# Other start addresses in SBUF for the split activations and the large region: two lead-in buffers and seven unused parameter columns

## The reference

```python
h = rmsnorm(x, mix_pre_g) * (1.0 + sc1) + sh1
proj = h @ w_in                                       # 1024 x 10272
y_ssd = ssd_branch(z, xbc, dt_raw, ...) @ w_ssd_out
y_sc = short_conv_branch(sc_b, sc_c, sc_h, sc_conv_w) @ w_sc_out
x = x + gt1 * rmsnorm((g_ssd * y_ssd + g_sc * y_sc) @ w_o, mix_post_g)
h = rmsnorm(x, ffn_pre_g) * (1.0 + sc2) + sh2
u_gate, u_val = jnp.split(causal_dwconv(h @ w_up, ffn_conv_w, ffn_conv_b), 2, axis=-1)   # 1024 x 5632
x = x + gt2 * rmsnorm((silu(u_gate) * u_val) @ w_down, ffn_post_g)                       # 2816 x 1024
...
x = x + gate_a * ((g_a * o_a + g_b * o_b) @ w_o)      # second layer: o_a, o_b are the two attentions
x = x + gate_f * ((silu(gt) * val) @ w_down)
```

## Time and profile before

| what | before |
|---|---|
| median of 3 runs | 1115.75 us (1113.66 to 1116.21) |
| time of the profiled execution | 1113.12 us |
| its span, as the profile shows it | 1111.3 us |
| TensorE matmul busy (PE) | 1051.7 us, 95% |
| weight loads (PEld) | 993.7 us, 89% |
| GpSimd (POOL) / ScalarE (ACT) / VectorE (DVE) busy | 692.6 / 642.6 / 562.8 us |
| mean granted TensorE clock | 0.986 of full |

### The profile page before, as it was taken

One profiled execution on the slowest core, in us unless ns is written; L12 is line 12 of the kernel. 1 busy time (PEld: TensorE's weight loads), 2 busy tenths in 40 slices (PEclk: granted clock), 3 DMA queues, 4 the chain that ended last, 5 costly groups with the idle time before them and its releaser, 6 DMA issues.

```text
span 1111.3 us, 22886 instructions
## 1 busy us (share of the span) xinstructions
PE 1051.7 (95%) x8357; PEld 993.7 (89%) x8357; DVE 562.8 (51%) x1165; ACT 642.6 (58%) x1140; POOL 692.6 (62%) x306
## 2 busy tenths in 40 slices
PE   3999999999899989999999999998998889999998
PEld 2999999988789979999998999896665689999998
DVE  5877425589774454555423432495263724444400
ACT  3555754477764576666546557735576546666532
POOL 0787888812268847888786487660220065888795
PEclk9999999999999999999999999999899999999999
DMA  9988677656427855676677387567211033555463
GB/s 372 380 283 287 245 292 285 224 184 209 168 99 268 263 204 171 228 242 223 217 258 252 110 286 278 174 206 293 98 40 38 1 117 129 195 186 188 162 208 106
DMA packets 63650, 226.84 MB, mean 204 GB/s; under 512 B 6976, under 2 KB 8160, under 8 KB 63328
## 3 DMA queue, kind: packets, MB, share of 16 engines
q1 hardware_dynamic: 62384, 221.74, 57.1%
q10 hardware_dynamic: 1200, 4.23, 1.3%
HBM read 224.86 MB, written 1.08 MB: 203 GB/s over the span
## 4 chain that ended last, share of the span: by engine, by line
PE 67%; issue 16%; POOL 8%; ACT 3%; DMA 2%; DVE 2%; SPq 1%; POOLq 0%; ACTq 0%; DVEq 0%
PE psL L550 64%; POOL WL L503 8%; DMA R<-ada_w 1%; PE psS L550 1%; PE psO L550 1%; DMA ring<-wts 1%; SPq L405 1%; ACT WH L1042 1%; ACT R L1153 0%; ACT L1033 0%; ACT HR L1074 0%; SPq L390 0%; POOL R L530 0%; PE psS L839 0%; DVE HR L1649 0%
## 5 line engine op out<-in xcount | busy, mean ns | idle before, releaser
L503 POOL TENSOR_TENSOR WL<-ring,WH 128x1024 fp32r<-128x1024 f32 (+1 forms) x282 | 672.2, 2398 | 306.4 <-ACT WH L1042 245.5
L550 PE MATMUL psL<-HR,WH 128*128 128x256 f32 x3056 | 545.4, 281 | 5.7 <-POOL WL L503 2.5
L550 PEld LDWEIGHTS psL<-HR,WH 128*128 128x128 f32 x3056 | 468.2, 188 | 10.3 <-POOL WL L503 4.4
L550 PE MATMUL psL<-HR,WL 128*128 128x256 f32 x1528 | 428.1, 280 | 0.0
L550 PEld LDWEIGHTS psL<-HR,WL 128*128 128x128 f32 x1528 | 288.3, 189 | 0.0
L1042 ACT ACTIVATE WH<-ring 128x1024 fp32r<-128x1024 f32 (+1 forms) x210 | 216.1, 1040 | 100.9 <-PE psL L550 84.5
L550 PE MATMUL psL<-RR,WH 128*128 128x256 f32 x1344 | 240.8, 282 | 6.1 <-POOL WL L503 4.5
L550 PEld LDWEIGHTS psL<-RR,WH 128*128 128x128 f32 x1344 | 206.9, 189 | 7.7 <-issue 3.9
L550 PE MATMUL psL<-RR,WL 128*128 128x256 f32 x672 | 188.8, 281 | 0.0
L1328 ACT ACTIVATE WH<-ring 128x1024 fp32r<-128x1024 f32 (+1 forms) x88 | 92.9, 1055 | 86.8 <-PE psL L550 86.8
L1909 DVE SCALAR_TENSOR_TENSOR CT<-psL,par,CT 128x254 f32<-128x254 f32 (+1 forms) x176 | 81.0, 480 | 116.7 <-ACT CT L1331 111.3
(11 more groups left out here) (255 smaller groups left out, 1103.5 us busy)
## 6 DMA issues: line engine op xcount, KB each, us to landing
ring<-wts SPq DMA_DIRECT2D x289, 512.0 KB, 3.7
adaring<-ada_w SPq DMA_DIRECT2D x80, 512.0 KB, 4.8
R<-ada_w SPq DMA_DIRECT2D x16, 512.0 KB, 12.6
ring<-wts SPq DMA_DIRECT2D x16, 384.0 KB, 3.4
R<-cum_dram ACTq DMA_DIRECT2D x8, 512.0 KB, 4.3
ring<-wts SPq DMA_DIRECT2D x8, 288.0 KB, 3.7
adaring<-wts SPq DMA_DIRECT2D x1, 2048.0 KB, 9.4
WHF<-wts SPq DMA_DIRECT2D x2, 1024.0 KB, 7.8
```

What stands on the lines that cost most here:

```text
L503: nc.gpsimd.tensor_tensor(WL[:, k, 0:n], ring[:, k, 0:n], WH[:, k, 0:n].bitcast(F32), SUB).then_inc(lo_done, 1)
L550: return nc.tensor.matmul(out, lhsT, rhs, start=start, stop=stop)
```

## The change

Two buffers that nothing reads or writes are declared, one ahead of `HR`/`HX` (16 columns, 64 bytes) and one ahead of `RR`/`R` (4 columns, 16 bytes), and `par` and the parameter array in HBM get seven columns of zeros at their end. No instruction is added, taken away or moved on any engine.

```diff
-    ("cmask_add", 2 * NCMP), ("cmask01", 2 * NCMP), ("sel", 2 * NCMP),
+    ("cmask_add", 2 * NCMP), ("cmask01", 2 * NCMP), ("sel", 2 * NCMP), ("pad", 7),
 ]
...
         X = sb("X", [P, KD, T])
         SQ = sb("SQ", [P, 2048])
+        sb("lead_in_h", [P, 16])
 
         with nc.sbuf_tensor("HR", [P, 4096], F32R) as HR:
             pass
         HX = sb("HX", [P, 4096])
+        sb("lead_in_r", [P, 4])
         with nc.sbuf_tensor("RR", [P, 22528], F32R) as RR:
             pass
         R = sb("R", [P, 22528])
...
         "sel": np.tile(np.eye(32, 2 * NCMP, dtype=np.float32), (4, 1)),
+        "pad": np.zeros((P, 7), np.float32),
```

## The result

The changed kernel takes 1117.85 us (median of 20 runs, 1113.05 to 1129.33), the kernel before 1112.28 us (median of 20, 17 more than the three shown ahead). One of the 20 runs before took 1304.80 us, and the ratio is taken without it; the others lie between 1107.13 and 1118.54. The ratio is 1.0053, with a 95% interval of 1.0027 to 1.0079: slower by half a per cent, where faster by 2.4% was forecast. The profiled execution took 1119.98 us with a span of 1118.2 us, 6.9 us more than the one before.

What follows compares the result with a forecast made beforehand. TensorE's matmul count times the distance between starts was taken as the bound; 28.9 us gained, less 1.7 for VectorE and 0.6 for GpSimd, gives 26.6 and, from the runs' median 1115.75, a forecast of 1089 us, range 1075 to 1119.

Steps and rivals of the forecast that it cites:

- What bounds the kernel: Long TensorE stretches: time is the number of matmuls, 6,600, times the distance between two starts, mostly 117.8 ns.
- why I take the nearer known value, the fast rhythm of 113.3, for both buffers: HR and RR matmuls at the new distances: 117.8 falls to 113.3 ns, 6504 times 4.44 ns, 28.9 us gained.
- Its lower bound: Distance per matmul is bounded from below by the weight load, 111 ns from ten matmuls on the block of ones.
- The rival "more": HR and RR matmuls: streams don't meet, weight load alone binds at some 111.6 ns; 1078 us, chance 0.08.
- tok2 was read: The long stretch in tok2, with HR loaded, runs at 113.3 ns; taken as the value for the new distances.
- the smallest case of "slower": Only today's fast stretches are lost, 96 matmuls in up1 and some 400 in tok2: 2.2 us, 1118 us.
- The rival "slower": All 6,600 matmuls: stream meets weight loads more often, a further 4.44 ns each, 29.3 us; 1145 us, chance 0.18.
- Its threshold: The slower case counts from 0.34 ns more per matmul, which makes 2.2 us.
- "No change": All stretches: rhythm depends on timing after a wait alone, addresses do nothing; 1115.75 us, chance 0.26.
- VectorE as the bound of the last part of in1: Last 16 units of in1: VectorE takes over as bound, pair period stays 3.83 us, 1.7 us of gain lost.
- The terms taken as nothing: par's seven columns, and VectorE, ScalarE, GpSimd and DMA work on the moved buffers: 0 each.
- The rule on ports: TensorE: separate read ports for moving operand and weight load, so address distance can't matter; sum 0, time 1115.75 us.

Runs made afterwards that it cites:

- at 112: HR and RR both placed 112 bytes past the weights (modulo 256), against the kernel before: 1091.32 us against 1108.31, ratio 0.9848.
- the sweep: Kernel before plus 38 unused 48-matmul stretches at its end, RR moving at varied distances from the weights, float32 matmul between; 113.35 ns at 64, 120.00 at 128.
- both at 192: HR and RR both placed 192 bytes past the weights (modulo 256), against the kernel before: 1091.54 us against 1113.8, ratio 0.9818.
- the sides swapped: Kernel before plus 40 unused stretches, RR loaded and weights streaming; after a wait 192 was fast in 6 of 8, 64 in 1 of 8.
- the weights moved: Weights moved to 0 modulo 256, HR and RR kept at 192, against the kernel before: 1096.79 us against 1105.98, ratio 0.9898.
- the separate starts after a wait: Kernel before plus 48 unused stretches, each after a ScalarE wait, at 64, 192, 128, 160; 64 always 117.8 ns, 192 fast in 8 of 12.

## Why the prediction was wrong

**What bounds the kernel** was right. 6,600 matmuls times the distance between two starts is what the time moves with, in both directions: 5.6 us more in the median, from 1 ns in HR's stretches and 5 in tok2, and at 112 22 us less of span.

**The step that failed** is "why I take the nearer known value, the fast rhythm of 113.3, for both buffers". For 128 and 160 there was no row, and nothing made 113.3 nearer to them than anything else in the range given. They have 118.7 (120.0 in a separate stretch) and 117.3 or 118.6. The term, a gain of 28.9 us, was in truth a loss of 4.4 for HR and a gain of about 0.1 for RR.

**Its lower bound was misread.** The ten rows on the block of ones, 111 ns apart, were taken for the weight load alone. They are float32 matmuls, and each of those stands in the profile as two rows: the sweep has one such matmul between stretches, and its timeline shows `x2` there. So 111 ns is half of a float32 matmul, and no run shows what the weight load alone would take. The rival "more" and the bound rested on it.

```profile
1148.37 0.38 PE L550 MATMUL psO<-par 128*128 128x128 f32 x2
```

**tok2 was read with the wrong consequence.** The prediction took from it that another distance than 64 would be fast. What it could have taken is which: swapping the sides turns 64 into 192, and at 192 the one long stretch was fast. The runs show that reading to hold, with both at 192, with the sides swapped and with the weights moved. The loss of today's fast stretches was named as the smallest case of "slower", 2.2 us; in tok2 it came, 2.2 us there alone, together with HR's 4.4.

**The rival "slower"** was the right one, with its mechanism, the stream meeting the weight loads more often. Its price was 29 us from a whole further step of 4.44 ns; the steps measured are 1 ns for HR, none for RR and 5 for tok2. That the loss is a meeting of the two streams is still argued, since no run takes the stream or the loads away. Its threshold, 0.34 ns on the mean, was passed by that.

**"No change"** was half right. At 64 and at 192 the start decides between the two rhythms, as the earlier trace rows suggested. The prediction held against this rival that chance would have to put every long stretch at 64 into the slow one. In its one trace chance did just that: over five traces 6 of the 15 longest were fast. So "HR or RR moving is slow" was in part one trace's luck, though at 64 slow is the rule (8 fast of 76 in the kernel, none of 12 in the separate starts after a wait) and at 192 fast is frequent (11 and 7 of 15, and 8 of 12). At no other distance was a stretch at 113.3 seen, except at 112, where with the activations moving it is the only one once settled. That also explains part of the kernel before's own spread: one long stretch of 1,488 is worth 6.6 us, and in one run it took 1090.54 us, at a clock (0.992) at which another took 1105.98. That this run had its long stretches fast is argued; it has no trace.

**VectorE as the bound of the last part of in1** was wrong by a little. The forecast held the period at 3.83 us; at 112 it is 236.69 - 232.93 = 3.76, so VectorE, although busy nearly all the time, had room to follow from pair to pair. At the end of the stage it is the bound after all: TensorE's wait for it grows from 0.3 to 1.2 us, so about half of the 1.7 us set aside is lost. GpSimd keeps up in the long stretches at 112, as forecast, and TensorE's waits for its splits grow from 7.0 to 7.9 us, near the 0.6 set aside. The waits in 229 to 300 us, before and at 112:

```profile
PE psO L550 <- DVE adaring L1796: 0.3, 1, 0.3
```

```profile
PE psO L560 <- DVE adaring L1806: 1.2, 1, 1.2
```

**The terms taken as nothing were nothing**: VectorE's busy time went from 562.8 to 562.9 us, ScalarE's from 642.6 to 642.5. The start of the long stretch in in1 (39.77 us before, 40.87 after) lay between 39.70 and 40.90 in kernels with the same addresses up to there, so that difference, 1.1 of the 6.9 us between the spans, can't be put down to the change.

**The rule on ports.** The Trainium skill, "TensorE: Matmul & The Clock Gate", Part 2, says that weight loads don't steal read bandwidth from a running matmul. The sweep has between 113.3 and 123.7 ns for the same 256 columns and the same loads, by nothing but the distance of their addresses. For this form of matmul the measurement decides against what the prediction drew from the rule, that the distance can't matter. Whether what is lost is read bandwidth, no run shows.

What stays open is the mechanism below: why 64, 112 and 192, and what about a start picks the rhythm. And in the kernel HR at 128 had 118.7 while the separate stretch behind a float32 matmul had 120.0; the start's part in that was seen, not taken apart further.

## What to carry to other kernels

Where matmuls with weight loads of their own follow on each other without a gap, the distance between two starts is the figure to read, and it can depend on where the moving operand begins relative to the stationary one. Measure that in one kernel, with stretches at every distance in steps of 16 bytes, before moving buffers, and start some of them after a real wait, since a distance can allow two rhythms. For the same reason take several traces of the kernel before: in one trace every long stretch at 64 had 117.8 ns, and in each of the next four at least one had 113.3. Here 112 bytes (modulo 256) gave 1.5% and steady runs, 192 gave 1.8% on the median but with spread, and 128 with 160 cost 0.5%. Compute the distance from the built addresses, since the rounding to 32 bytes made 160 out of a counted 144.

## What was unexpected of the hardware

- With every size the same, the distance between starts of matmuls of 256 columns ran from 113.3 to 123.7 ns with the operands' distance modulo 256; distances that aren't multiples of 16 bytes were never under 117.6.
- At 64 and 192 two rhythms are stable over hundreds of matmuls (113.3 and 117.8 ns, 1,488 matmuls in 168.94 or in 175.53 us), and the start after a wait picks one. With all of the kernel's own buffers at the same addresses, up1 with down1 took 168.92 us in one trace and 175.53 in another. At 112 all starts with the activations moving ended in the fast one.
- The time of the changed kernel, at whose distances no stretch was seen in the fast rhythm, still went from 1113.05 to 1129.33 us over 20 runs, with the mean granted clock (0.992 to 0.977).
- Moving both operands by 64 bytes left the rhythm as it was (168.96 and 168.97 us for 1,488 matmuls); moving the activations alone changed it, and moving the weights alone changed how often it is fast.
